# Reading the moving operand of the projections as pairs of words 256 apart

## The reference

```python
# first block
proj = jnp.einsum('bld,dn->bln', rmsnorm(x, norm_g), w_in)      # 2048 -> 14336
v, bg, cg, za, u, zb, ga, gb = jnp.split(proj, SPLITS, axis=-1)
ya = bg * causal_depthwise_conv(cg * v, conv_w)
ya = jnp.einsum('blc,cd->bld', ya * jax.nn.silu(za), w_out_a)
yb = jax.nn.gelu(s5_scan(u, ...))                                # complex diagonal state space
yb = yb * jax.nn.sigmoid(jnp.einsum('blc,ce->ble', yb, w_glu) + b_glu)
yb = jnp.einsum('blc,cd->bld', yb * jax.nn.silu(zb), w_out_b)
m = jax.nn.sigmoid(ga) * ya + jax.nn.sigmoid(gb) * yb
x = rmsnorm(x + jnp.einsum('bld,de->ble', m, w_o), final_g)
# second block
h = rms_norm(x, norm_g[l]) * (1.0 + scale) + shift               # from cond @ w_ada
u_a, v_a, g_a, q_b, k_b, v_b, g_b, f_b = jnp.split(h @ w_in[l], pts, axis=-1)
y_a = chunked_spatial_gating(gelu(u_a), gelu(v_a), ...) * silu(g_a)
y_b = forgetting_attention(q_b, k_b, v_b, f_b, b_f[l]) * silu(g_b)
x = rms_norm(x + gate * (jnp.concatenate([y_a, y_b], -1) @ w_out[l]), final_g)
```

## Time and profile before

| | |
|---|---|
| time, median of 3 runs | 2667.86 us (2667.31 to 2668.21) |
| the profiled execution, its own time | 2670.03 us |
| its span | 2668.8 us |
| TensorE busy (matmuls) | 2631.5 us, 99% of the span, 11928 instructions |
| TensorE weight loads | 2159.8 us, 81% |
| DVE | 1638.4 us, 61% |
| ACT | 845.1 us, 32% |
| POOL | 390.9 us, 15% |
| mean granted TensorE clock | 0.993 of full speed |
| DMA | 353.07 MB, mean 132 GB/s |

### The profile page before, as it was taken

The page is one execution under the profiler, slowest core; times in us unless marked ns, Lnnn a source line. Parts: engine busy times, 40 slices in busy tenths (PEclk is TensorE's granted clock), DMA queues, the critical chain, the costliest instruction groups (busy, mean ns, idle before and its releaser), DMA issues.

```text
span 2668.8 us, 30016 instructions
## 1 busy us (share of the span) xinstructions
PE 2631.5 (99%) x11928; PEld 2159.8 (81%) x11928; DVE 1638.4 (61%) x2187; ACT 845.1 (32%) x1139; POOL 390.9 (15%) x295
## 2 busy tenths in 40 slices
PE   9989999999999999999999999999999999999997
PEld 7878888888888888888888888877888888888786
DVE  6678888787887765445444775556465563234434
ACT  5122222222222222222322332332565563233321
POOL 0034343433443421000000000010000000000001
PEclk9999999999999999999999999989999999999999
DMA  5233333333333333667555675623222222322333
GB/s 184 96 112 112 105 114 99 121 110 104 116 103 125 128 121 120 215 202 245 186 193 192 207 240 181 197 95 129 95 80 73 86 80 87 111 95 87 115 122 111
DMA packets 119867, 353.07 MB, mean 132 GB/s; under 512 B 15408, under 2 KB 22832, under 8 KB 119728
## 3 DMA queue, kind: packets, MB, share of 16 engines
q1 hardware_dynamic: 119728, 351.16, 39.7%
HBM read 321.68 MB, written 23.07 MB: 129 GB/s over the span
## 4 chain that ended last, share of the span: by engine, by line
PE 96%; DVE 2%; issue 1%; POOL 0%; ACT 0%; DMA 0%; SPq 0%; DVEq 0%; POOLq 0%; ACTq 0%
PE bank L512 29%; PE bank L513 28%; PE bank L514 28%; PE bank L678 2%; PE bank L680 2%; PE bank L679 2%; PE bank L721 1%; PE bank L711 1%; PE bank L576 1%; PE bank L564 1%; DVE X L1814 0%; PE bank L704 0%; PE bank L702 0%; PE bank L502 0%; DMA W<-in_w 0%
## 5 line engine op out<-in xcount | busy, mean ns | idle before, releaser
L1138 DVE TENSOR_TENSOR WL<-W,WH 128x1024 fp32r<-128x1024 f32 (+1 forms) x456 | 592.2, 1301 | 528.3 <-ACT WH L816 527.0
L816 ACT ACTIVATE WH<-W 128x1024 fp32r<-128x1024 f32 (+1 forms) x456 | 480.6, 1056 | 1008.6 <-PE bank L514 768.8
L512 PE MATMUL bank<-hH,WH 128*128 128x512 f32 x1792 | 700.3, 391 | 10.7 <-DVE WL L1138 6.8
L513 PE MATMUL bank<-hL,WH 128*128 128x512 f32 x1792 | 699.1, 390 | 0.0
L514 PE MATMUL bank<-hH,WL 128*128 128x512 f32 x1792 | 698.8, 390 | 0.0
L512 PEld LDWEIGHTS bank<-hH,WH 128*128 128x128 f32 x1792 | 337.1, 188 | 89.9 <-DVE WL L1138 7.2
L514 PEld LDWEIGHTS bank<-hH,WL 128*128 128x128 f32 x1792 | 337.1, 188 | 70.6
L513 PEld LDWEIGHTS bank<-hL,WH 128*128 128x128 f32 x1792 | 337.2, 188 | 70.2
L512 PE MATMUL bank<-h2H,WH 128*128 128x512 f32 x640 | 252.6, 395 | 0.1
L514 PE MATMUL bank<-h2H,WL 128*128 128x512 f32 x640 | 249.4, 390 | 0.0
L513 PE MATMUL bank<-h2L,WH 128*128 128x512 f32 x640 | 249.1, 389 | 0.0
(11 more groups left out here) (260 smaller groups left out, 3604.5 us busy)
## 6 DMA issues: line engine op xcount, KB each, us to landing
W<-in_w SPq DMA_DIRECT2D x335, 512.0 KB, 3.7
W<-in_ada SPq DMA_DIRECT2D x96, 512.0 KB, 4.4
W<-in_wa SPq DMA_DIRECT2D x32, 512.0 KB, 3.9
W<-in_wo SPq DMA_DIRECT2D x32, 512.0 KB, 3.9
W<-in_wvv SPq DMA_DIRECT2D x32, 512.0 KB, 3.7
W<-in_wb SPq DMA_DIRECT2D x16, 512.0 KB, 3.7
URAW<-U SPq DMA_DIRECT2D x96, 64.0 KB, 3.1
scr_am<-SO SPq DMA_DIRECT2D x16, 256.0 KB, 2.0
```

The costliest lines, as they stand in the source:

```text
L512: e.matmul(o, wh, xh, start=first, stop=False)
L513: e.matmul(o, wh, xl, start=False, stop=False)
L816: e.activation(WH[:, n % NB, c], W[:, i % NW, c], ACT.Copy).then_inc(sem["hi"], 1)
L1138: e.tensor_tensor(WL[:, s, c], W[:, plan.item_of[n] % NW, c], WH[:, s, c].bitcast(F32), ALU.subtract).then_inc(sem["lo_v"], 1)
```

## The change

Three views are added. `pairs(x)` turns a row of 512 words into the order 0, 256, 1, 257, 2, 258, and so on to 511. It is used for the moving operand of every projection matmul of 512 columns, of `drive` and of the small matmul for the forget logits (`fps`). Column 2b + a of the bank then holds token 256a + b (in `seq`, output channel 256a + b). So each eviction reads its bank through `tokens`, as two runs of 256 words with a step of two words, and sees the other operands and the result through `halves`, the same 512 words in their old place as two runs of 256. What lies in SBUF after an eviction is the same as before.

Not changed are the stationary operands, the weight loads, the order in which any engine does its work, the waits, the DMAs, the matmuls of the scores, of attention's values, of the transposes, of the sums, of `readout` and `mix`, and the 96 matmuls of 256 columns of the last projection.

```diff
+    def pairs(x):
+        return x.rearrange("p (a b) -> p b a", a=2)
+    def tokens(b):
+        return b.rearrange("p (b a) -> p a b", a=2)
+    def halves(x):
+        return x.rearrange("p (a b) -> p a b", a=2)
...
-                mm = triple(bank[b][:, :], WH[:, s, c], WL[:, s, c], XH(k), XL(k), k == k_first, k == k_last)
+                mm = triple(bank[b][:, :], WH[:, s, c], WL[:, s, c], pairs(XH(k)), pairs(XL(k)),
+                            k == k_first, k == k_last)
...
-                    mm = e.matmul(bank[b + z][:, :], BSTK[:, s, z, :], USTK[:, s, :], start=True, stop=True)
+                    mm = e.matmul(bank[b + z][:, :], BSTK[:, s, z, :], pairs(USTK[:, s, :]), start=True, stop=True)
...
-                    wh, wl = WH[:, s, 512 * k2:512 * k2 + 512], WL[:, s, 512 * k2:512 * k2 + 512]
+                    wh, wl = (pairs(w[:, s, 512 * k2:512 * k2 + 512]) for w in (WH, WL))
...
-            mm = triple(fps, WFH[:, k, :], WFL[:, k, :], h2H[:, k, :], h2L[:, k, :], k == 0, k == 15)
+            mm = triple(fps, WFH[:, k, :], WFL[:, k, :], pairs(h2H[:, k, :]), pairs(h2L[:, k, :]), k == 0, k == 15)
...
-                    e.activation(T[:, 0, :], bank[bank_of[p]][:, :], ACT.Copy).then_inc(sem["a_a"], 1)
+                    e.activation(halves(T[:, 0, :]), tokens(bank[bank_of[p]][:, :]), ACT.Copy).then_inc(sem["a_a"], 1)
...
-                br, bi = bank[4 + 2 * (j % 2)][:, :], bank[5 + 2 * (j % 2)][:, :]
+                br, bi = (tokens(bank[4 + 2 * (j % 2) + z][:, :]) for z in range(2))
...
-                e.tensor_tensor(v[0], c, br, ALU.mult).then_inc(sem["ssm_v"], 1)
+                e.tensor_tensor(halves(v[0]), halves(c), br, ALU.mult).then_inc(sem["ssm_v"], 1)
...
-            e.tensor_tensor(SO[:, s % 2, :], bank[bank_of[p]][:, :], RSA[:, :], ALU.mult).then_inc(sem["sp_v"], 1)
+            e.tensor_tensor(halves(SO[:, s % 2, :]), tokens(bank[bank_of[p]][:, :]), halves(RSA[:, :]),
+                            ALU.mult).then_inc(sem["sp_v"], 1)
...
```

More of the change, by code:

```diff
@@ L935, in act_program @@
             o = T[:, g % 2, :]
-            e.activation(o, bank[bank_of[p]][:, :], ACT.Sigmoid,
+            e.activation(halves(o), tokens(bank[bank_of[p]][:, :]), ACT.Sigmoid,
                          bias=col["bglu"][:, g:g + 1]).then_inc(sem["g_a"], 1)
@@ L969, in seq_read @@
                     projected(seq_p[i])
-                e.activation(dst[:, q, 512 * part:512 * part + 512], bank[SEQ_BANKS[q]][:, :],
+                e.activation(halves(dst[:, q, 512 * part:512 * part + 512]), tokens(bank[SEQ_BANKS[q]][:, :]),
                              func).then_inc(sem["sv"], 1)
@@ L1034, in act_program @@
                     for hh in range(2):
-                        src = b[rows[hh], :]
-                        e.activation(QA[rows[hh], buf, hh, :], src, ACT.Copy, scale=0.125).then_inc(sem["q_a"], 1)
-                        e.activation(QB[buf][0:64, hh, :], src, ACT.Copy, scale=0.125).then_inc(sem["q_a"], 1)
+                        src = tokens(b[rows[hh], :])
+                        e.activation(halves(QA[rows[hh], buf, hh, :]), src, ACT.Copy,
+                                     scale=0.125).then_inc(sem["q_a"], 1)
+                        e.activation(halves(QB[buf][0:64, hh, :]), src, ACT.Copy,
+                                     scale=0.125).then_inc(sem["q_a"], 1)
                 elif i == 1:
@@ L1063, in gates @@
             o = T[:, h % 2 + 2 * i, :]
-            e.activation(o, bank[bank_of[p]][:, :], ACT.Silu if i else ACT.Gelu).then_inc(sem["ug_a"], 1)
+            e.activation(halves(o), tokens(bank[bank_of[p]][:, :]), ACT.Silu if i else ACT.Gelu).then_inc(sem["ug_a"], 1)
         for h in range(4):
@@ L1424, in keep_u @@
             projected(u_p[m])
-            e.tensor_tensor(U[:, m, :], bank[bank_of[u_p[m]]][:, :], RSA[:, :], ALU.mult).then_inc(sem["u_rd"], 1)
+            e.tensor_tensor(halves(U[:, m, :]), tokens(bank[bank_of[u_p[m]]][:, :]), halves(RSA[:, :]),
+                            ALU.mult).then_inc(sem["u_rd"], 1)
         for m in range(2, 8):
@@ L1468, in dve_program @@
                     e.wait_ge(*nth("a_v", c, 5))
-                    e.tensor_tensor(o, o, bank[bank_of[p]][:, :], ALU.mult).then_inc(sem["a_v"], 1)
+                    e.tensor_tensor(halves(o), halves(o), tokens(bank[bank_of[p]][:, :]),
+                                    ALU.mult).then_inc(sem["a_v"], 1)
                 if i == 3:
@@ L1506, in dve_program @@
             projected(p)
-            e.tensor_tensor(MA[:, d, :], bank[bank_of[p]][:, :], gate_in(at_load), ALU.mult).then_inc(sem["ma"], 1)
+            e.tensor_tensor(halves(MA[:, d, :]), tokens(bank[bank_of[p]][:, :]), halves(gate_in(at_load)),
+                            ALU.mult).then_inc(sem["ma"], 1)
             at_load += 1
@@ L1594, in forget @@
             e.wait_ge(*nth("res", 15))
-            ts(F, x, fps, col["bf"][0:16, 0:1], None, ALU.add)
+            ts(F, halves(x), tokens(fps), col["bf"][0:16, 0:1], None, ALU.add)
             stt(F, a, x, -1.0, x, ALU.mult, ALU.min)
@@ L1693, in dve_program @@
                         e.wait_ge(*nth("q_a", j, 2 * hh + 2))
-                        e.scalar_tensor_tensor(out=QA[rows[1 - hh], buf, hh, :], in0=b[rows[hh], :], scalar=0.125,
-                                               in1=QA[rows[hh], buf, hh, :].bitcast(F32), op0=ALU.mult,
+                        e.scalar_tensor_tensor(out=halves(QA[rows[1 - hh], buf, hh, :]), in0=tokens(b[rows[hh], :]),
+                                               scalar=0.125, in1=halves(QA[rows[hh], buf, hh, :].bitcast(F32)),
+                                               op0=ALU.mult,
                                                op1=ALU.subtract).then_inc(sem["q_v"], 1)
@@ L1799, in dve_program @@
             at_load += 1
-            e.scalar_tensor_tensor(out=X2[:, d, :], in0=bank[bank_of[p]][:, :], scalar=MOD[:, 32 + d:33 + d],
-                                   in1=si, op0=ALU.mult, op1=ALU.add).then_inc(sem["x_v"], 1)
+            e.scalar_tensor_tensor(out=halves(X2[:, d, :]), in0=tokens(bank[bank_of[p]][:, :]),
+                                   scalar=MOD[:, 32 + d:33 + d], in1=halves(si), op0=ALU.mult, op1=ALU.add).then_inc(sem["x_v"], 1)
             e.wait_ge(*nth("x_a", d))
```

24 lines of the change are left out of this document (13 added, 11 removed).

## The result

| | before | after |
|---|---|---|
| median | 2668.03 us (2667.31 to 2669.73, 4 runs) | 2550.83 us (2550.25 to 2552.88, 4 runs) |
| ratio | | 0.9561, 95% interval 0.9545 to 0.9578 |
| span of the profiled execution | 2668.8 us | 2551.6 us |

The change takes 117 us off, 4.4%. Forecast were 2558 us and a range of 2521 to 2720.

What follows compares the result with a forecast made beforehand. TensorE was taken as the bound, matmul count times 226.7 ns between starts. From 2670.0 us, less 109.6 for the moving read, plus 0.1, came 2560.5; the median stands 2.2 lower, so 2558 us, range 2521 to 2720.

Steps and rivals of the forecast that it cites:

- What sets the 226.7 ns: Start-to-start distance of 512-column matmuls: 13.3 ns above the columns' 213.3 at full clock, none at half; moving read likely.
- The size: Moving read of 10,960 matmuls: 10 ns gained on each, 109.6 us in all; bounds 146 us gain to 2192 us loss.
- the 128-column pair: Scores of a head: two matmuls start 0.06 us apart where columns take 0.053, so about 3 ns seems to stay.
- The reason I gave: Moving read at full clock: reading two places in turn can start or run ahead as one run can't; 10 ns gain.
- The excess goes by matmul, not by word: Last projection's 256-column matmuls: 119.3 ns against 106.7 of columns, again about 13 ns despite half as many columns.
- Evictions at no cost: Strided bank reads, 320 on DVE and 128 on ACT: zero added; upper bound 613 ns each on DVE, 457 on ACT.
- Rival C: Evictions cost as twice the words, moving read unchanged: late low parts WL add 45 us, 2713 us; chance 0.09.
- Rival A: Order of the moving words doesn't matter: excess comes from starting a read, stays 226.7 ns, 2668 us; chance 0.28.
- Waits: TensorE's waits for low part WL: stay at one of some 7 us, so the gain should come through whole.
- The range: Forecast's own range: 2521 us with all of the excess gone to 2597 us with half of it; chance 0.44.
- Rival B: Moving read gets slower: each word needs its own fetch, 426.7 ns per matmul, +2192 us, some 4860 us; chance 0.19.

Runs made afterwards that it cites:

- e1: Against the change: moving operands still read as pairs, evictions read their banks in order (tokens in wrong order); 2551.27 us, ratio to before 0.9564.
- e2: Against the change: evictions still read every second word, moving operands back to one run of 512 (tokens in wrong order); 2667.75 us, ratio to before 0.9998.
- p1: Small kernel without the computation: 48 matmuls in a row in each of 21 ways; 226.7 ns for one run, 215.8 ns for pairs 256 apart.

## Why the prediction was right

- *What sets the 226.7 ns.* The forecast rested on this step: an excess of 13.3 ns that is there at full clock and not at half clock belongs to the supply, not to the array. It held: e1 against e2 shows that the order of the moving read sets it, with weight loads and writes to the bank the same. p1 shows that no other engine is needed for it (226.7 ns with nothing beside), nor a long weight load (16 columns: 231.6 ns).
- *The size.* I took 10 ns of the 13.3, leaving about 3 because the 128-column pair seemed to keep that much. Measured were 10.9 ns in a plain stretch, leaving 2.5, and 11.2 ns over the kernel. The term came to 122 us instead of 109.6, and 5 us of waits and half-clock stretches, which the sum didn't have, took part of it back: 2670.0 - 122 + 5 = 2553 us, against a measured 2552.9 for the profiled execution. So the error of 7 us is the difference of two smaller ones. That the 3 ns came out near 2.5 is in part luck: they rest on one distance of 0.06 us, rounded to 0.01.
- *The reason I gave was only half right.* I wrote that two places read in turn can start or run ahead in a way that one run can't. Two places alone don't do it: two runs of 256 stand at 227.9 ns, four places at 283 ns, 16 words from each half in turn at 240 ns. By the model of two lanes, what does it is that each lane takes four words from its line instead of two. The reason as given would have spoken for those orders just as well, so it was luck that this order is one of those that gain.
- *The excess goes by matmul, not by word.* True of one run (119.7, 174.0 and 226.7 ns for 256, 384 and 512 columns, each some 13 to 14 ns above the columns' own time), and true of the pairs at 384 and 512 (162.4 and 215.8, 2.4 and 2.5 above). Pairs of 256 columns keep 5 ns (111.7 against 106.7), near the 111 ns at which 128 columns stand with their weights. Why a lane that takes two words from a line loses 13 ns a matmul and not something per word isn't settled.
- *Evictions at no cost.* Right: 320 on DVE and 128 on ACT, each group's mean unchanged to within 4 ns. Rival C had its price from a row with twice the words, and the step of two words doesn't count as that.
- *Rival A* would have had 2668 us. It spoke for itself with the excess being the same for 256 and 512 columns, "as a cost of starting would be". The excess behaves so, and still the order sets it. I had counted that fact for A and against B and not asked whether it excluded my own case; it didn't.
- *Waits.* I expected the waits for WL to stay at one of some 7 us. They became three, 8.6, 1.1 and 0.4 us. In e1, with evictions in order, they are the same three, and in e2 one of 6.7 us, so they come with the faster stream and not with the strided evictions. The gain thus didn't come through quite whole.
- *The range.* Half of the excess is 73 us, which gives 2595 us by the same sum, not 2597. Nothing else hangs on it.
- *Rival B* is real, for other orders than this one: every second word takes 451 ns and pairs in steps of four words 453 ns, twice the time of the change, about as B priced it (427). Its mechanism was that neighbouring words come two by two in one fetch and that taking them apart costs a fetch each. In the change's order, by the model of two lanes, each lane still empties its line.
- *The Trainium skill's rule* on lines of 16 bytes ("SBUF — State Buffer", section "Door 1: The DMA port swizzle") spoke for B. Read for the order as a whole it is contradicted here: in the pairs no word follows another from the same line, and they are the fastest of all. Read for each lane it fits the orders that the model covers in that one hit a line takes 451 to 461 ns, two 226.7 ns and four 215.8 ns; but by the rule two hits should be enough, and here they already fall short of full rate. For warm starts the Trainium skill ("TensorE: Matmul & The Clock Gate", section "Wait — 56ns, not 53.3ns?") has 215.7 ns for two-byte operands; the trace agrees for them (216.1 ns) and shows that four-byte operands reach the same only in pairs.

## What to carry to other kernels

Where a stream of fp32r matmuls bounds the kernel, compare the distance between their starts with the columns' own time at full and at half clock: here the excess stood at full clock alone, and the order of the read took 10.9 of its 13.3 ns away. For four-byte moving operands read the row as pairs at least four words apart (4 to 260 were tried) that begin on a 16-byte line (here 4.4% of the whole kernel), and put the order right in the evictions, where a step of two words was free. Try it on 48 matmuls by themselves first: the neighbours of this order cost up to twice the time, and for two-byte operands the same order does (484 ns for 216).

## What the runs showed of the hardware that was not expected

- A plain run of neighbouring four-byte words isn't the fastest moving read: 226.7 ns for 512 columns against 215.8 for pairs. For words of two bytes no order tried was faster (216.1 as one run, 215.8 in the best).
- Four-byte words of a moving operand behave in most orders as if they went through two lanes by even and odd place, each with a 16-byte line: 4, 2 and 1 words per line give 215.8, some 227 and 451 to 461 ns. That is a model which foretold the three orders that set it apart. It fails where a lane goes back and forth between two places: runs of 2 and four places it would put near 452 ns (340 and 283 measured), runs of 4 and of 16 at 226.7 ns (250 and 240 measured). What the memory does in fact isn't shown.
- One run is slower when it begins off a boundary: 236.6 ns from word 1, 233.4 from word 8, 232.2 from word 32, 226.7 from word 128, 256 or 512. Pairs 256 to 260 apart stood between 215.8 and 216.7 ns from any start that was tried (word 0, 1, 2, 4 and 64); pairs 4 apart lost the gain from word 2 (226.9).
- ACT and DVE read every second word of a bank at the speed of a run (600 and 597 ns, 690 and 689 ns).
- DVE's writing of the low part WL takes 1321 to 1326 ns beside the faster stream and 1302 to 1304 ns beside the slower one, in seven traces. The cause isn't shown.
